# A fused two-layer attention trunk: scores of the next block moved behind both heads' transposes and the values, with moves of single instructions elsewhere

## What is computed

```python
u = rmsnorm(h, norm_g)
proj = u @ w_in                      # q, k, v, g of 8 stick-breaking heads; q, k, v, g of the window heads
# stick-breaking, 64 wide, per block of 128 queries against all keys up to it:
z = q @ k.T / 8
log_beta = log_sigmoid(z)
log_1m = where(causal, log_beta - z, 0)
tail = cumsum(log_1m, reverse=True) - log_1m
a = where(causal, exp(log_beta + tail), 0)
sb_o = (a @ v) * silu(g_sb)
# sliding window of 128 in chunks of 64, rotary positions, 8 query heads on 2 key heads, learned sinks
sw_o = softmax_with_sink(rope(q) @ rope(k).T) @ v * silu(g_sw)
h = h + concat(sb_o, sw_o) @ w_out
```

## Time and profile before

| | us |
|---|---|
| median of 3 runs | 1213.29 |
| lowest and highest | 1212.85, 1214.43 |
| the profiled execution | 1215.04 |
| its span | 1213.2 |
| busy PE in that span | 1174.4 (97%) |
| busy weight loads (PEld) | 1074.2 (89%) |
| busy DVE | 688.3 (57%) |
| busy ACT | 435.8 (36%) |

### The profile page before, as it was taken

How to read it: one execution, slowest core, us unless ns; L and a number is a source line. 1 busy time by engine, 2 the same in 40 slices (tenths; PEclk the granted TensorE clock), 3 DMA queues, 4 the chain that set the end, 5 groups by cost and what they waited for, 6 DMA issues and landing times.

```text
span 1213.2 us, 22513 instructions
## 1 busy us (share of the span) xinstructions
PE 1174.4 (97%) x8922; PEld 1074.2 (89%) x8922; DVE 688.3 (57%) x1370; ACT 435.8 (36%) x1189; POOL 2.6 (0%) x5
## 2 busy tenths in 40 slices
PE   6999999999999999999989999999999999999998
PEld 6988888988888888899989888888888888888998
DVE  6646464455457567754574564655544855766533
ACT  7323333333344344521231333333334433554113
POOL 0000000000000000000000000000000000000000
PEclk9999999999999999999999999999999999999999
DMA  6611010101021021141321110101011212104203
GB/s 213 219 36 36 19 36 18 36 19 36 21 56 44 23 57 50 41 172 35 141 70 54 34 36 19 36 19 36 18 36 25 64 36 45 49 14 171 70 5 140
DMA packets 101687, 69.31 MB, mean 57 GB/s; under 512 B 37824, under 2 KB 95168, under 8 KB 101584
## 3 DMA queue, kind: packets, MB, share of 16 engines
q1 hardware_dynamic: 100720, 66.55, 18.2%
q10 hardware_dynamic: 864, 1.32, 0.4%
HBM read 49.82 MB, written 12.71 MB: 52 GB/s over the span
## 4 chain that ended last, share of the span: by engine, by line
PE 89%; DVE 5%; issue 2%; ACT 2%; DMA 1%; SPq 0%; ACTq 0%; DVEq 0%
PE psum L867 41%; PE psum L855 20%; PE psum L917 7%; PE psum L946 6%; PE psum L929 6%; PE psum L978 2%; PE psum L1043 1%; PE psum L990 1%; PE psum L1015 1%; PE psum L1008 1%; DVE mix L1382 1%; DMA vT<-in_x 1%; PE psum L959 1%; PE psum L888 1%; DVE UL L1392 1%
## 5 line engine op out<-in xcount | busy, mean ns | idle before, releaser
L867 PE MATMUL psum<-UH,WH 128*128 128x384 f32 (+2 forms) x1632 | 538.5, 330 | 10.1 <-DVE UL L1392 4.9
L867 PE MATMUL psum<-UL,WH 128*128 128x384 f32 (+2 forms) x1632 | 524.6, 321 | 0.0
L855 PE MATMUL psum<-UH,WL 128*128 128x384 f32 (+2 forms) x1632 | 517.9, 320 | 0.0
L867 PEld LDWEIGHTS psum<-UH,WH 128*128 128x128 f32 x1632 | 308.4, 189 | 19.9 <-issue 9.0
L867 PEld LDWEIGHTS psum<-UL,WH 128*128 128x128 f32 x1632 | 309.1, 189 | 0.1
L855 PEld LDWEIGHTS psum<-UH,WL 128*128 128x128 f32 x1632 | 308.3, 189 | 0.0
L1255 ACT ACTIVATE PT<-psum 128x512 f32<-128x512 f32 (+5 forms) x260 | 116.7, 492 | 20.0 <-PE psum L929 18.3
L1246 ACT ACTIVATE X<-psum 128x264 f32<-128x264 f32 (+9 forms) x240 | 91.1, 431 | 78.2 <-PE psum L917 77.8
L1514 DVE TENSOR_TENSOR_SCAN X<-X,stick 16x16 f32<-16x16 f32 (+5 forms) x144 | 100.4, 736 | 24.7 <-ACT X L1246 24.3
L929 PE MATMUL psum<-ident,X 128*128 128x128 f32 x576 | 91.1, 283 | 3.7 <-ACT Vn L1209 2.7
L1517 DVE TENSOR_TENSOR_SCAN X<-X 128x352 f32<-128x352 f32 (+4 forms) x96 | 86.3, 939 | 7.7 <-ACT X L1246 7.7
(11 more groups left out here) (171 smaller groups left out, 1000.7 us busy)
## 6 DMA issues: line engine op xcount, KB each, us to landing
w_raw<-in_w_in SPq DMA_DIRECT2D x36, 512.0 KB, 3.8
h_spill<-X SPq DMA_DIRECT2D x16, 520.0 KB, 6.5
X<-h_spill SPq DMA_DIRECT2D x16, 520.0 KB, 5.2
w_raw<-in_w_in SPq DMA_DIRECT2D x32, 256.0 KB, 3.7
w_raw<-in_w_out SPq DMA_DIRECT2D x16, 256.0 KB, 2.9
w_raw<-in_w_out SPq DMA_DIRECT2D x32, 128.0 KB, 3.2
vT<-dvT SPq DMA_DIRECT2D x40, 50.0 KB, 2.0
vT<-dvT SPq DMA_DIRECT2D x40, 48.0 KB, 2.0
```

The costliest lines, as they stand in the source:

```text
L855: return pe.matmul(out_columns, WL[:, j % 2, k, :], UH[:, k, uses], start=False, stop=(k == KT - 1))
L867: pe.matmul(out_columns, WH[:, j % 2, k, :], u[:, k, uses], start=(k == 0 and u is UH), stop=False)
```

## The change

In `sb_attention` the list of a group's parts changes. Before, a group is two parts, the transposes of head 0, and the transposes of head 1 with the lagged values; the scores of the next block are spread over the parts and each share stands ahead of its part. After, a group is one part, both transposes and the lagged values, and each share of the next block's scores stands behind its part. The fill is merged by the same rule as before.

The other moves:

- Window attention: the scores of the first two units stand ahead of the first fill tasks, with the last lagged values of the stick-breaking stage ahead of all. Weight splits of the input tiles go from behind a unit's values to behind the next unit's transposes.
- Start of layer 0: the squares of blocks 4 to 8 go one step later, split_w 1 is done as two steps (high and low), and the norm row of group 1 goes into the first projection. Layer 1 also splits tile 1 in two steps.
- Layer boundary: norm 1 stands in chunk 0's pieces, the split of the next layer's first tile is two steps with the last pieces of chunk 0 between, and the first projections of layer 1 wait for the addition that used their bank, not for the last addition of the layer.
- End: the sum of squares of chunk 2 goes between the two halves of the turn of block 7, and each block of the output leaves as two DMAs of half its columns, each waiting for the engine that made that half.

The lists below are the instructions of an engine in order; a name in square brackets is what an instruction waits for, and xN stands for N alike in a row.

The diff, cut to its core:

```diff
-    spread = {c0[0]: [S[4]], c0[2]: [S[5]], c0[4]: [C[4]], c0[5]: [S[6]], c0[7]: [C[5]], c0[8]: [S[7]], c0[10]: [S[8]]}
+    spread = {c0[2]: [S[4]], c0[4]: [C[4]], c0[5]: [S[5]], c0[7]: [C[5]], c0[8]: [S[6]], c0[10]: [S[7], S[8]]}
     for step in c0:
         steps += [step] + spread.get(step, [])
-    steps += [C[6], ("in_root", 1), ("in_refine", 1)] + v[0] + [T[8], ("in_row", 1), ("in_row", 2), ("split_w", 1)]
-    spread = {c1[1]: [C[7]], c1[6]: g[0], c1[8]: [C[8]]}
+    steps += [C[6], ("in_root", 1), ("in_refine", 1), ("split_w", 1, "high")] + v[0] + [T[8], ("in_row", 2)]
+    spread = {c1[1]: [("split_w", 1, "low"), C[7]], c1[6]: g[0], c1[8]: [C[8]]}
     for step in c1:
...
-            start = [("split_w", 1)] + v[0] + c1[:4] + [("norm", 2, 0)] + c1[4:7] + g[0] + c1[7:]
+            start = [("split_w", 1, "high")] + v[0] + c1[:3] + [("split_w", 1, "low")] + c1[3:4] + [("norm", 2, 0)]
+            start += c1[4:7] + g[0] + c1[7:]
...
                turns = [("T", p, b, 0, tiles), ("T", p, b, 1, tiles)]
                 done = [("AV", p, b, tiles, n == 0)] + ([("AV_rest", p, b)] if 4 * n + 4 >= b else [])
-                values += [turns[:1], turns[1:] + lagged([], done)]
+                values.append(turns + lagged([], done))
 
             ahead = scores[b + 1] if 1 <= b and b + 1 < BLOCKS else []
             out.append(("R", p, b))
             for i, part in enumerate(values):
-                out += ahead[-(-i * len(ahead) // len(values)):-(-(i + 1) * len(ahead) // len(values))] + part
+                out += part + ahead[-(-i * len(ahead) // len(values)):-(-(i + 1) * len(ahead) // len(values))]
...
-        out = fill[0] + [("SZ", 0), ("SD", 0)] + fill[1] + [("SZ", 1)]
-        fill = fill[2:]
+        out = [("SZ", 0), ("SD", 0)] + fill[0] + [("SZ", 1)] + fill[1]
+        fill, weights_next = fill[2:], []
         for n in range(len(UNITS)):
             task = fill.pop(0) + (fill.pop(0) if n == 0 else [])
             late = [step for kind in ("rope_add", "split_w") for step in task if step[0] == kind]
@@ -226,12 +227,13 @@
             if n + 1 < len(UNITS):
                 out.append(("SD", n + 1))
             out += [("ST", n, part) for part in (("main", "meta") if UNITS[n][1] != META_UNIT else ("meta",))]
-            out += extra.get(n, []) + ropes + [step for step in task if step not in late + ropes]
+            out += extra.get(n, []) + ropes + weights_next + [step for step in task if step not in late + ropes]
             if n + 2 < len(UNITS):
                 out.append(("SZ", n + 2))
             elif n + 1 == len(UNITS):
                 out.append(("add", 1, 0))
-            out += [("SAV", n)] + late
+            weights_next = [step for step in late if step[0] == "split_w" and step[1] <= IN_TILES]
+            out += [("SAV", n)] + [step for step in late if step not in weights_next]
             if n == len(UNITS) - 2:
...
     tail[-1] = tail[-1] + flat(window[30:])
-    tail[0] = flush + tail[0]
-    steps += swa_attention(tail + [[("proj", IN_TILES + i, c)] for i, c in EARLY_OUTS])
+    steps += flush + swa_attention(tail + [[("proj", IN_TILES + i, c)] for i, c in EARLY_OUTS])
 

...
             (KT - 2, 1): c0[:5],
-            (KT - 1, 1): c0[5:],
-            (KT - 2, 2): [("norm", 1, 1), ("split_w", TILES)]}.get((i, c), [])
+            (KT - 1, 1): c0[5:8] + [("norm", 1, 1), c0[8]],
+            (KT - 2, 2): [("split_w", TILES, "high")] + c0[9:] + [("split_w", TILES, "low")]}.get((i, c), [])
...
             (KT - 2, 2): [("out_sum", 1), ("out_root", 1)] + blocks(4, 7),
-            (KT - 1, 2): [("out_turn", 7), ("out_sum", 2), ("out_root", 2), ("out_copy", 7)] + blocks(8, 9)}.get((i, c), [])
+            (KT - 1, 2): [("out_turn", 7), ("out_root", 2), ("out_copy", 7)] + blocks(8, 9)}.get((i, c), [])
 
 
 
 WITHIN = {("proj", TILES - 2, 1): {4: [("norm", 0, 1)], 7: [("norm_row", 0, 1)]},
           ("proj", TILES - 2, 2): {5: [("norm", 1, 1)]},
-          ("proj", 0, 0): {4: [("norm_row", 1, 0), ("in_turn", 6)], 6: [("in_turn", 7)]},
+          ("proj", 0, 0): {4: [("norm_row", 1, 0), ("in_turn", 6)], 6: [("in_turn", 7)], KT + 5: [("in_row", 1)]},
...
             for b in range(1, BLOCKS):
                 sp.wait_ge(out_ready_a, b)
+                sp.dma_start(out[128 * (b - 1):128 * b, 0:512], staged_out(b)[:, 0:512]).then_inc(out_stored, 16)
                 sp.wait_ge(out_ready_v, b)
-                sp.dma_start(out[128 * (b - 1):128 * b, :], staged_out(b)).then_inc(out_stored, 16)
-            sp.wait_ge(out_stored, 16 * (BLOCKS - 1))
+                sp.dma_start(out[128 * (b - 1):128 * b, 512:1024], staged_out(b)[:, 512:1024]).then_inc(out_stored, 16)
+            sp.wait_ge(out_stored, 32 * (BLOCKS - 1))
...
                     elif l:
-                        pe.wait_ge(h_ready.sem, h_ready.at(l, 0))
+                        pe.wait_ge(h_ready.sem, h_ready.at(l, use - 1))
...
                         for k in range(KT):
+                            if l == 0 and KT + k in WITHIN.get(step, {}):
+                                in_rows(1)
                             ins = pass_low(k)
...
+                        if b == 7 and half == 0:
+                            out_sums(2)
...
-                def split_w(j):
-                    dve.wait_ge(w_landed[j % 2].sem, w_landed[j % 2].at(l + j // TILES, landed(j % TILES)))
-                    if j >= 2:
-                        dve.wait_ge(proj_full.sem, proj_full.at(l, PROJ_AT["proj", j - 2, 2] + 1))
-                    if l or j >= 2:
-                        dve.wait_ge(wl_made.sem, wl_made.at(l, j - 1))
-                    dve.tensor_copy(WH[:, j % 2, :, :], w_raw[:, j % 2, :, :]).then_inc(wh_made.sem, 1)
-                    if l or j:
+                def split_w(j, part=None):
+                    if part != "low":
+                        dve.wait_ge(w_landed[j % 2].sem, w_landed[j % 2].at(l + j // TILES, landed(j % TILES)))
+                        if j >= 2:
+                            dve.wait_ge(proj_full.sem, proj_full.at(l, PROJ_AT["proj", j - 2, 2] + 1))
+                        if l or j >= 2:
+                            dve.wait_ge(wl_made.sem, wl_made.at(l, j - 1))
+                        dve.tensor_copy(WH[:, j % 2, :, :], w_raw[:, j % 2, :, :]).then_inc(wh_made.sem, 1)
+                    if (l or j) and part != "high":
                         dve.wait_ge(wh_made.sem, wh_made.at(l, j + 1))
                         dve.wait_ge(wl_made.sem, wl_made.at(l, j))
```

More of the change, by code:

```diff
@@ L757, in _ @@
                 for step in LAYER_STEPS[l]:
-                    if step[0] == "split_w" and step[1] + 2 < TILES:
+                    if step[0] == "split_w" and step[1] + 2 < TILES and step[2:] != ("high",):
                         load(step[1] + 2)
@@ L1657, in _ @@
                     elif kind == "split_w":
-                        split_w(step[1])
+                        split_w(*step[1:])
                     elif kind == "norm":
```

## The result

The changed kernel takes 1258.24 us (median of 4 runs, 1257.05 to 1258.64) against 1213.86 of before: a ratio of 1.0364, with a 95% interval of 1.0346 to 1.0382. That is 44 us slower. The forecast was 1269, between 1244 and 1289. The mean granted clock of the profiled execution fell from 0.994 to 0.982.

The account below looks back on a forecast made before the run. The prediction took TensorE (PE), busy 97%, to bound the kernel. Its terms, 43 waits + 0 banks + 20 clock - 3 boundary - 4 window = +56 on the median 1213.3, gave 1269 us, range 1244 to 1289.

Parts of the forecast that it names:

- main case: Whole kernel: waits at 18 places plus falls of the clock, less gains elsewhere, +56 to 1269 us; chance 0.62.
- first rival: Whole kernel: the 18 waits come as priced but the clock holds, 1249 us; chance 0.22.
- The waits behind scores: Stick-breaking stage: transposes directly behind their own block's scores wait for scans at nine places per layer, +43 us.
- The rotary place: Pair 3, block 5: scan queued behind the rotary addition's DMA wait; 6.5 us, plus 0.2 for head 1, per layer.
- The clock: PE behind the new waits: 14 falls to 1.2 GHz at 1.4 us each, +20 us, ends 0 and 25.
- Banks: Scores and transposes waiting for banks: give-backs against new waits in block 4, taken as 0, ends -15 and +8.
- Boundary: First projection of layer 1: shorter wait for the residual addition, -3 us, ends 0 and -4.6.
- Window: Window attention: earlier first scores may remove waits on early weights and queries, -4 us, ends 0 and -4.1; moved splits hidden.
- Tail: Kernel's end: small matmuls between two transposes and output in halves change nothing, ends -1 and +1.
- the rotary addition did not spread: Rival: pair 3's DVE delay makes two more places per layer wait 6.5 us each, 1295 us; chance 0.08.
- The faster one: Rival: PE waits only 0.7 us a place, so the give-backs win, 1202 us; chance 0.05.
- that of no change: Rival: chunks' cover mostly remains, waits of 1.3 us a place cancel the gains, 1213 us; chance 0.03.

Follow-up runs that it names:

- e2_only_scores: The kernel before with only the list of the stick-breaking stage changed to the new one: 1269.49 us, ratio 1.0465.
- e5_rope: The changed kernel with each layer's first rotary addition moved behind the last scan of pair 3's block 5: 1252.88 us, ratio 1.0320.
- e7_wait_alone: The kernel before with layer 1's first projection waiting for the addition that used its bank, not the layer's last: 1211.02 us, ratio 0.9976.
- e8_window_alone: The kernel before with only the window attention's start changed (first scores and last lagged values earlier), weight splits not moved: 1211.12 us, ratio 0.9975.
- e1_old_scores: The changed kernel with the stick-breaking stage's list put back as before, all other moves kept: 1205.72 us, ratio 0.9938.
- e1_again: The changed kernel with the old stick-breaking list and all other moves, measured once more: 1206.25 us, ratio 0.9930.

## Why the prediction was right, and where its terms were off

The time alone does not choose between the main case and the first rival: 1258.24 is 11 under the one (1269) and 9 over the other (1249). What was right is the mechanism, transposes that wait for their own scans at the 18 places named; of the falls of the clock, fewer came than forecast.

**The waits behind scores** were forecast at 43 and are 36.7 for the 18 places (38.4 with all waits of transposes on scans). The first-head figures came out of the earlier trace rows within 0.05: 1.45 against 1.47, 1.7 against 1.65 and 1.70, 1.3 against 1.30. That held because sigmoid and scan start when the scores end, in either order. What was too much is the second head's share: the 18 places should have cost 5 us for it, and the waits of transposes on scans hold only 1.7 beyond the 18. The rotary place was 6.5 in the forecast and is 5.97.

**The clock** was the term that was mis-sized: +20 from 14 falls. PE's busy time rose by 8.9, with falls at 6 of the 18 places and two elsewhere (544.2, 684.1), and falls of before at 73.9, 463 and 613 gone. The price of a fall, 1.4, nearly held (1.4 to 1.7): with the same two waits, a pair of heads in after took 83.8 us without a fall (pair 1, layer 0), 85.4 with one (pair 2, layer 0) and 86.5 with two (pair 1, layer 1), from its first scores to the next pair's. The range of the term (0 to 25) held the result too; the count, 14, did not follow from the rows. The runs show that it can't be had from the length of a wait: the 16 waits outside pair 3's block 5 are alike within 0.01 us in after, e2_only_scores and e5_rope, and 4, 6 and 9 of them had a fall. The first rival, waits without falls, fails too, as in each of them some of the 1.47 us waits were followed by 1.2 GHz. The Trainium skill, "TensorE: Matmul & The Clock Gate", section "HAM oscillation — how this bites in real kernels", ties falls to waits for DMA longer than the matmul work between them. Of the 18 places only the two rotary ones hang on a DMA, and both had a fall; but four others had one as well, as at 110.7 behind a wait of 1.47 us that no DMA ended, so in this trace such waits are not the only cause.

**Banks**, taken at 0: scores wait 4.1 us longer at PE, and transposes 1.1 less for v's copies (3.7 before, 2.6 after): +3.0. Block 4's price of the earlier trace rows was close (0.63 against 0.56).

**Boundary**, -3: the first matmul of layer 1 waits 3.18 us less, and 0.58 for the norm's small steps came in its place, 2.6 in all. The wait on the low parts of chunk 1 stayed at 1.02, where the prediction had it grow. e7_wait_alone shows the wait's half of the gain; the other half is the difference to after.

**Window**, -4: 2.9 us of waits on the early weights and 1.4 on the queries went, 4.3 in all, but 2.1 came later in the stage: 1.3 for the low parts of a weight tile and 0.8 for the residual additions, so -2.2. That moving the splits is hidden was wrong. The wait for low parts stands in the list of every kernel with the moved splits and in none of before, e2_only_scores, e7_wait_alone and e8_window_alone. In after DVE ended that split at 529.2, and PE waited until then:

```profile
529.25 0.45 PE L857 MATMUL psum<-UH,WL 128*128 128x400 f32 x1 [0.63 <-DVE WL L1441]
```

In before the split at that place ended on DVE at 505.8, and PE came to its low part only at 508.55.

**Tail**, 0: it gained 0.85. The span of before ended 3.4 us after its last DMA was issued (at 1209.80), that of after 2.55 us later (1254.15); the last piece is half as large.

```profile
1254.15 0.33 SPq L772 DMA_DIRECT2D out<-w_raw  x1
```

**Start**, 0: PE's waits there are 1.3 us shorter (1.0 for a row of the first norm, 0.3 for low parts). That need not be the moves: the first of them is 0.2 us in e1_old_scores and 0.9 in e1_again, which are one program.

The sum as it is, by the same terms: 38.4 + 3.0 + 8.9 - 2.6 - 2.2 - 0.85 - 1.3 = 43.35, against 43.5 by which the span grew. Of the 12.5 us between the forecast's +56 and the span's 43.5, 11.1 are the clock and 4.6 the second heads and the rotary place, less 3.0 for the banks; the rest nearly cancels.

The rivals: the rotary addition did not spread (no other wait above 1.74 in pair 3). The faster one, and that of no change, failed at their point of 1.3 us a place: the places cost 2.0 us on average (36.7 / 18) before any clock, and the shortest 1.30.

## What to carry to other kernels

Price a moved instruction by what it waits for, from the old trace: the latency of a producer's chain (here sigmoid and scan, 1.3 to 1.7 us) is there even where no wait shows it, and it shows as soon as nothing covers it. A new order and its cover are two things: the same list cost 55 us without a chunk in 18 gaps, and was 11.5 us better than the old one once the gaps were filled, what stood in the queues behind them moved, and block 4's two score steps set apart. When a step waits for a DMA on an engine that works in order, look at what is queued behind it there, and then at the next engine.

## What was not expected of the hardware

Identical waits had falls of the granted clock in one kernel and not in another: behind 1.70 us at one place none in after (88.40 to 91.80 at 1.00) and one in e2_only_scores (0.51). The 18 waits of after and of e2_only_scores are alike within 0.01 us, and 6 against 8 had a fall; with the waits on scans cut by 8.1 us in e5_rope there were 11, and PE's work took 3.2 us longer. Nor is it only a matter of the kernel: e1_old_scores and e1_again are the same program, and behind the start the profiled execution of the first had no fall before its last us, that of the second had two (at 518.0 and 658.0), with 1169.6 and 1173.0 us of busy PE. So 3 us of clock come and go between two executions of one kernel, and a difference of that size between two profiles can't be put down to a move; the runs don't settle what decides.
